# Another order and other banks for the up products, and halved first down products, in the MLP stage of a hybrid decoder layer

## What is computed

```python
h = rms_norm(x, norm_mlp[l])
x = x + jnp.square(jax.nn.relu(h @ w_up[l])) @ w_down[l]
```

## Time and profile before

| | us |
|---|---|
| median of 2 runs | 889.94 (889.81 to 890.07) |
| profiled execution | 885.3 |
| its span | 883.5 |
| PE busy | 786.3 (89%) |
| DVE, POOL, ACT busy | 535.6, 472.9, 370.2 |
| mean granted clock of PE | 0.944 |

### The profile page before, as it was taken

The page is one execution under the profiler, slowest core; times in us unless marked ns, Lnnn a source line. Parts: engine busy times, 40 slices in busy tenths (PEclk is TensorE's granted clock), DMA queues, the critical chain, the costliest instruction groups (busy, mean ns, idle before and its releaser), DMA issues.

```text
span 883.5 us, 13102 instructions
## 1 busy us (share of the span) xinstructions
PE 786.3 (89%) x5122; PEld 670.4 (76%) x5122; DVE 535.6 (61%) x697; ACT 370.2 (42%) x604; POOL 472.9 (54%) x328
## 2 busy tenths in 40 slices
PE   8999999999999999999867789777897778977788
PEld 6888779887878887888767767676677766877666
DVE  6793788666855663547844766266652666325666
ACT  5202834564145554224254643345423453244531
POOL 5666446674566665666962625444344343553444
PEclk9999999999999999999979789898898988989889
DMA  7253222324211003324874968659486585965734
GB/s 275 74 177 110 97 75 73 119 97 167 96 49 48 26 24 120 143 96 167 235 194 110 244 177 209 153 145 239 127 212 148 142 240 124 231 163 125 191 62 129
DMA packets 37647, 124.40 MB, mean 141 GB/s; under 512 B 4259, under 2 KB 5035, under 8 KB 37588
## 3 DMA queue, kind: packets, MB, share of 16 engines
q1 hardware_dynamic: 24108, 81.06, 26.1%
q0 software_dynamic: 9360, 34.08, 21.0%
q10 hardware_dynamic: 4120, 8.44, 2.7%
HBM read 119.35 MB, written 5.26 MB: 141 GB/s over the span
## 4 chain that ended last, share of the span: by engine, by line
PE 66%; DVE 15%; ACT 7%; DMA 5%; issue 5%; POOL 1%; ACTq 1%; DVEq 0%; SPq 0%; POOLq 0%
PE bank L664 10%; PE bank L666 10%; PE bank L665 10%; DVE wsp L2079 4%; PE bank L1170 4%; PE bank L1171 4%; PE bank L1172 4%; DMA wraw<-in_w 4%; PE bank L1138 3%; ACT wsp L1551 3%; PE bank L1140 3%; PE bank L1141 3%; PE bank L1011 2%; PE bank L1044 2%; PE bank L1056 2%
## 5 line engine op out<-in xcount | busy, mean ns | idle before, releaser
L1138 PE MATMUL bank<-ghi,wsp 128*128 128x256 f32 x432 | 133.0, 308 | 63.0 <-DVE v_up L2096 23.8
L592 POOL TENSOR_TENSOR wsp<-wraw,wsp 128x1024 fp32r<-128x1024 f32 x44 | 118.2, 2731 | 99.9 <-ACT wsp L1551 99.8
L1551 ACT ACTIVATE wsp<-wraw 128x1024 fp32r<-128x1024 f32 x86 | 90.7, 1055 | 163.4 <-PE bank L1172 73.6
L515 POOL TENSOR_TENSOR wsp<-wraw,wsp 128x1024 fp32r<-128x1024 f32 x60 | 148.0, 2466 | 5.0
L664 PE MATMUL bank<-hhi,wsp 128*128 128x512 f32 x352 | 140.9, 400 | 2.0 <-DVE hlo L1651 1.1
L1138 PEld LDWEIGHTS bank<-ghi,wsp 128*128 128x128 f32 x432 | 92.0, 213 | 65.7 <-issue 52.1
L666 PE MATMUL bank<-hhi,wsp 128*128 128x512 f32 x352 | 137.4, 390 | 0.0
L665 PE MATMUL bank<-hlo,wsp 128*128 128x512 f32 x352 | 137.1, 390 | 0.0
L1140 PE MATMUL bank<-glo,wsp 128*128 128x256 f32 x432 | 130.7, 302 | 0.0
L1141 PE MATMUL bank<-ghi,wsp 128*128 128x256 f32 x432 | 130.4, 302 | 0.0
L513 POOL TENSOR_SCALAR wsp<-wraw 128x1024 fp32r<-128x1024 f32 x60 | 65.3, 1088 | 119.9 <-PE bank L666 107.1
(11 more groups left out here) (332 smaller groups left out, 1476.6 us busy)
## 6 DMA issues: line engine op xcount, KB each, us to landing
wraw<-in_w SPq DMA_DIRECT2D x126, 512.0 KB, 4.1
wraw<-in_w POOLq DMA_DIRECT2D x49, 512.0 KB, 7.3
raw<-in_w SPq DMA_DIRECT2D x16, 512.0 KB, 5.5
raw<-in_w POOLq DMA_DIRECT2D x15, 512.0 KB, 7.2
bias_skewed<-bias_lines ACTq DMA_DIRECT2D x1, 2048.0 KB
bias<-bias_skewed ACTq DMA_DIRECT2D x1, 2048.0 KB, 8.9
out<-fin SPq DMA_DIRECT2D x8, 256.0 KB, 2.1
x<-in_xT SPq DMA_DIRECT2D x3, 512.0 KB, 6.2
```

The lines of the kernel that those rows point to most:

```text
L515: pool.tensor_tensor(wlo[:, two, :], wraw[:, raw, :], whi[:, two, :].bitcast(F32), ALU.subtract).then_inc(w_split, 1)
L592: pool.tensor_tensor(lo, place, hi.bitcast(F32), ALU.subtract).then_inc(pool_low, 1)
L1138: pe.matmul(out_, hi[:, c], ghi[:, k, g, :], start=start and pp == 0 and k == 0, stop=False, skip_group_check=True)
L1551: act.activation(split_slot(n)[0], place, ACT.Copy).then_inc(split_hi, 1)
```

## The change

- The up products of a half go in the order S1, A11, S3, S2, A12, A22, S4, into banks named Z, X, W, Y, X, Y, Z. T3's product has a bank of its own (W) and T4's adds to Y. Z and W change places between the halves (banks 0 and 2). The sums become v = p1 - Y, p1 = W - v, u22 = p1 + Z, u12 = p1 + Y, s4 = v - Z; the first three come together after unit 3.
- The steps that need sums of the X chain (S1, S2, S4) are now units 0, 3 and 6.
- The down products begin with three products by their first halves (b11, t1, t3), then their second halves; the other four stay as they were. `take_off` counts in `c_read`, and the first down product waits for that count.
- The last group of forms is split in two (`GROUPS`), and VectorE's low parts of the forms of half 0 are moved into its work for half 1, those of half 1 behind it.
- POOL adds the next quarter's first X sum ahead of the last down sums, and Y later; it takes other low parts. VectorE makes only one low part of the next quarter before it keeps t4.
- At the start ScalarE issues the first three loads instead of SyncE and makes the high parts of steps 0 to 3, which POOL did (L590); POOL makes the low parts of steps 0 and 1 between the last `wo` weights. The low part of the activations' forms (`g_low`) comes ahead of the sum of squares for n of 4 or more.

```diff
-UP_FORMS = ["A11", "S1", "S2", "A12", "S3", "A22", "S4"]
-UP_PRODUCTS = [("X", "B11", True), ("Z", "T1", True), ("Y", "T2", True), ("X", "B21", False), ("Y", "T3", False),
-               ("W", "T4", True), ("Z", "B22", False)]
+UP_FORMS = ["S1", "A11", "S3", "S2", "A12", "A22", "S4"]
+UP_PRODUCTS = [("Z", "T1", True), ("X", "B11", True), ("W", "T3", True), ("Y", "T2", True), ("X", "B21", False),
+               ("Y", "T4", True), ("Z", "B22", False)]
-GROUPS = [(0, 1), (1, 3), (3, 7)]
+GROUPS = [(0, 1), (1, 3), (3, 5), (5, 7)]
+DOWN_UNITS = ([(m, half) for half in range(2) for m in range(3)] + [(m, half) for m in range(3, 7) for half in range(2)])
-GROUP_OF = {"u11": 0, "s1": 1, "s3": 1, "s4": 2, "s2": 2, "u12": 2, "u22": 2}
+GROUP_OF = {"u11": 0, "s1": 1, "s3": 1, "s4": 2, "s2": 2, "u12": 3, "u22": 3}
-POOL_LOWS = [0, 3, 4, 5, 7, 10, 11, 12] + [UP_N + 2 * SPLITS.index(part) + half for part in ("b11", "b22", "b21")
-                                            for half in range(2)]
+POOL_LOWS = [1, 2, 4, 5, 8, 9, 11, 12] + [UP_N + DOWN_UNITS.index((SPLITS.index(part), half))
+                                          for part in ("b11", "b22", "b21") for half in range(2)]
...
-        up_bank = dict(zip("XYZW", (bank[0], bank[1], bank[2], bank[3])))
+        up_bank = [dict(zip("ZXWY", (bank[0], bank[1], bank[2], bank[3]))), dict(zip("ZXWY", (bank[2], bank[1], bank[0], bank[3])))]
...
-            sp.wait_ge(w_used, AT["ab7"] + 1)
-            load_raw(0, 0, "X", up_chunk(0, 0, "O1"))
-            sp.dma_start(s1_first[:], up_chunk(0, 0, "O1")).then_inc(first_landed, 16)
-            load_raw(0, 0, "Y", up_chunk(0, 0, "O1"))
...
+                if c == N_STRAIGHT - 6:
+                    pool.wait_ge(first_landed, 16)
+                    pool.dma_start(s1_first[:], up_chunk(0, 0, "O2"), accum_op=ALU.add).then_inc(first_added, 16)
+                if c == N_STRAIGHT - 5:
+                    add_to(0, 0, "X", 1, up_chunk(0, 0, "O2"))
+                if c == N_STRAIGHT - 4:
+                    add_to(0, 0, "Y", 1, up_chunk(0, 0, "E1"))
+                if c == N_STRAIGHT - 3:
+                    low(0)
+                if c == N_STRAIGHT - 2:
+                    low(1)
...
                     n = STEPS * q + 7 * d
-                    low(n)
-                    if n == 0:
-                        low(1)
-                        low(2)
-                    else:
-                        after_low(n + 1, q, d, "X", 2, up_chunk(q, d, "E1"))
                     if n:
-                        low(n + 3)
-                    after_low(n + 2, q, d, "X", 3, up_chunk(q, d, "E2"))
+                        after_low(n, q, d, "X", 2, up_chunk(q, d, "E1"))
+                        low(n + 1)
+                    low(n + 2)
                     if n == 0:
                         low(3)
                     if d == 0:
-                        first_up_sums(q, 1)
+                        up_pair(q, 1, "X")
+                        up_pair(q, 1, "Y")
+                    after_low(n + 3, q, d, "X", 3, up_chunk(q, d, "E2"))
+                    if d:
+                        down_pair(q, 0, "b12")
+                        down_pair(q, 0, "x")
                     low(n + 4)
                     low(n + 5)
...
+                for half in range(2):
+                    after_low(step_of(q, "t3", half), q, half, "x", 2, part_chunk(q, "b11", half))
+                    low(step_of(q, "b22", half))
+                if not end:
+                    up_pair(q + 1, 0, "X")
+                for half in range(2):
+                    after_low(step_of(q, "t2", half), q, half, "x", 3, part_chunk(q, "b21", half))
+                    if end and half == 0:
+                        pool.wait_ge(b_read, 3 * q + 1)
+                        end_sum(sum5, ALU.subtract)
+                    if not end and half == 1:
+                        up_pair(q + 1, 0, "Y")
+                    low(step_of(q, "b21", half))
...
+                if i == 1 and big:
+                    pe.wait_ge(relu_d, 4 * big - 2)
+                if i == 2 and d:
+                    pe.wait_ge(up_sums, 5 * big)
+                if i == 2 and q and not d:
                     pe.wait_ge(b_read, 3 * q)
-                if i == 3:
+                if i == 4:
                     pe.wait_ge(p1_kept, big + 1)
-                done = {1: 5 * big, 2: 5 * big - 3, 4: 5 * big + 1, 5: 5 * big - 1, 6: 5 * big + 3}.get(i, 0)
-                if done > 0:
-                    pe.wait_ge(up_sums, done)
+                if i == 5:
+                    pe.wait_ge(up_sums, 5 * big + 1)
+                if i == 6:
+                    pe.wait_ge(up_sums, 5 * big + 3)
...
+                for m, half in DOWN_UNITS:
+                    if m == 2 and half == 0:
+                        pe.wait_ge(up_sums, 5 * (2 * q + 2))
+                    if m == 3 and half == 0:
+                        pe.wait_ge(c_read, 2 * q + 1)
...
+                if n in (2, 3, 6, 7):
+                    high({2: 0, 3: 1, 6: 2, 7: 3}[n])
...
+                    if n:
+                        high(n + 3)
                     high(n + 4)
                     if d:
                         high_of_group(q, 0, 1)
+                    act.wait_ge(w_used, used(n + 1))
+                    if big:
+                        act.wait_ge(up_sums, 5 * big - 1)
+                    act.activation(p1_up[:], up_bank[d]["X"][:], ACT.Copy).then_inc(p1_kept, 1)
                     high(n + 5)
                     if d:
                         high_of_group(q, 0, 2)
                     high(n + 6)
+                    if d:
+                        high_of_group(q, 0, 3)
+                    if big == 0:
                         act.wait_ge(m_stat, 1)
...
-                low(n + 4)
+                low(n + 3)
+                if d:
+                    low_of_group(q, 0, 1)
+                    low_of_group(q, 0, 2)
+                low(n + 6)
+                dve.wait_ge(w_used, used(n + 3))
                 dve.wait_ge(p1_kept, big + 1)
                 dve.tensor_tensor(v_up[:], p1_up[:], y_[:], ALU.subtract).then_inc(up_sums, 1)
-                low(n + 6)
-                low_of_group(q, d, 0)
-                dve.wait_ge(w_used, used(n + 4))
-                dve.tensor_tensor(p1_up[:], y_[:], p1_up[:], ALU.subtract).then_inc(up_sums, 1)
+                dve.wait_ge(up_sums, 5 * big + 1)
+                dve.tensor_tensor(p1_up[:], w_[:], v_up[:], ALU.subtract).then_inc(up_sums, 1)
...
+                low(n + 7)
+                if d:
+                    low_of_group(q, 0, 3)
                     low(n + 8)
+                low_of_group(q, d, 0)
+                if d:
+                    low(n + 9)
...
-                low_of_group(q, d, 1)
-                low_of_group(q, d, 2)
...
+                low_of_group(q, 1, 1)
                 low(step_of(q, "t1", 1))
-                low(step_of(q, "t3", 0))
+                low(step_of(q, "t3", 1))
+                low_of_group(q, 1, 2)
+                low_of_group(q, 1, 3)
                 keep(q, "b11", "a", sum_v, a_read, first=q == 0, scaled=False)
-                low(step_of(q, "t3", 1))
                 keep(q, "t1", "c", sum5, c_read)
...
                 if not end:
-                    low(n + STEPS + 1)
-                    low(n + STEPS + 2)
+                    low(n + STEPS)
                     keep(q, "t4", "b", sum4, b_read)
```

More of the change, by code:

```diff
@@ L627, in _ @@
                     if d == 0:
[L628 removed]
+                        up_pair(q, 1, "X")
[4 more added lines that the diff above has]
+                        down_pair(q, 0, "x")
                     low(n + 4)
                     low(n + 5)
[L631 to L643 removed]
+                down_pair(q, 1, "b12")
+                low(step_of(q, "b11", 0))
+                down_pair(q, 1, "x")
+                low(step_of(q, "b11", 1))
+                for half in range(2):
[11 more added lines that the diff above has]
+                    low(step_of(q, "b21", half))
             end_sum(sum4, ALU.add)
@@ L1526, in _, with high @@
             link(act.activation(minus_g, g_mlp, ACT.Copy, scale=-1.0))
+            act.wait_ge(w_used, AT["ab7"] + 1)
+            act.dma_start(s1_first[:], up_chunk(0, 0, "O1")).then_inc(first_landed, 16)
+            for role in ("X", "Y"):
+                s = slot_of(0, 0, role)
+                act.dma_start(raw_slots[s], up_chunk(0, 0, "O1")).then_inc(m_landed[s], 16)
+            def high(n):
+                if n >= STEPS * QUARTERS:
+                    return
+                place, there = raw_of(n)
+                act.wait_ge(*there)
+                act.wait_ge(w_used, slot_free(n))
+                act.activation(split_slot(n)[0], place, ACT.Copy).then_inc(split_hi, 1)
             for n in range(KT):
@@ L2064, in _ @@
                 g_forms(n)
+                if n >= 4:
+                    g_low(n)
                 dve.wait_ge(x2_sq, 4 + n + 1)
```

191 lines of the change are left out of this document (74 added, 117 removed).

## The result

The changed kernel takes 853.89 us (median of 2 runs, 853.23 to 854.55) against 889.94: a ratio of 0.9595 (95% interval 0.9554 to 0.9636), 36 us less. The profiled execution took 853.2, its span 851.1 (883.5 before), with PE 780.8 us busy (92%) and a mean granted clock of 0.964 (0.944).

A forecast was written before the change was run, and what follows sets the result against it. The MLP stage was taken as bound by PE's waits: a quarter of 79.0 plus 16.6 pauses and 5.8 slow clock, 101.4 against 108.8. Three quarters save 22.2, the first loses 4.0: 18.2 less, 871 us, range 854 to 888.

The forecast's parts named there:

- A: New pause before unit 5 of half 0, v waiting behind S4's low part and the third X sum: 3.0 us.
- E: New pause before b22, waiting for keep t1 behind the forms' last low parts on VectorE: 4.4 us.
- P1: Old pause of 6.46 us before unit 1 of half 0, behind keep t4; forecast to go.
- P3: Old pause of 3.73 us before unit 1 of half 1, waiting for s4's sum; forecast to go, 0.3 left.
- P5: Old pause of 3.76 us before the second half of t1, behind the forms' low parts; forecast to go.
- B: New pause before unit 3 of half 1, S2's low part late on VectorE after meeting GpSimd's low parts: 5.4 us.
- P4: Old pause of 6.29 us before unit 4 of half 1, waiting for v behind a forms' low part and `take_off`.
- C and D: Estimated pauses: 1.4 us before unit 5 of half 1; 2.4 before the second halves of b11, t1 and t3.
- R1: Rival: VectorE's and GpSimd's low parts mostly don't meet; quarter 92, total 844, or 857 with half the meetings gone; chance 0.21.
- R2: Rival: sums share DMA engines with SP's loads, the third X sum lands 3 us later; total 881; chance 0.18.
- R3: Rival: pauses only move, the quarter stays at 108 to 109; total 889 to 893; chance 0.10 shared with another rival.
- R4: Rival, slower: the third X sum lands 17 us after issue, delaying v; total 896; chance 0.07.

The follow-up runs named there:

- e16: Changed kernel with whole first down products and the low parts of half 0's forms back where the kernel before had them: 859.1 us.
- e12: Changed kernel with the low parts of s1, s3 and the third group of half 0's forms back ahead of half 1's first low parts: 867.9 us.
- e9: Changed kernel with the moves of e3, e6 and e8 together: 807.5 us.
- e2: Kernel before, with VectorE keeping t4 ahead of the low part of the next quarter's S2: 885.7 us.
- e15: Kernel before, with the low parts of half 0's second and third group of forms behind v and S4's low part of half 1: 889.8 us.
- e13: e9 with GpSimd's low part of unit 4 of half 1 ahead of three sums for the down products: 817.6 us.
- e11: Kernel before with two moves: keep t4 ahead of S2's low part, and S4's low part behind the sum u22: 904.5 us.
- e3: Changed kernel with v, W - v and u22 of half 0 ahead of S4's low part on VectorE: 835.2 us.
- e6: Changed kernel with half 0's third X sum issued ahead of half 1's first two sums: 831.3 us.
- e8: Changed kernel with the low part of the third group of half 1's forms behind the keeps of b11 and t1: 838.5 us.

## Why the prediction was wrong

The sign, the new long pauses A and E and the end of P1, P3 and P5 were right; the sum of a quarter, and so the total, was too high. The largest term that failed is pause B. By its steps:

- **P1 and P3 go, A comes.** Held: A is 3.6 to 4.0 (3.0 taken, 1.8 to 4.7 allowed) with the chain as forecast; the sum was 11.3 on its way where 10 was taken. v was ready 18.2 after unit 0 began (553.35 to 571.54), where the working had 16.5; that the 3.0 came close owes something to its being taken 1.1 above the working's own 1.9. In e16 the same exchange is 11.2 us of P1 to P3 for an A of 3.8 to 6.4, some 17 of its 28 us over three quarters.
- **B, the step that failed.** 5.4 was forecast and 1.35 to 1.47 measured. The working put u11's low part behind both of GpSimd's, 5.0 long; VectorE got in between them and it took 2.49 (2.48 and 2.49 in the other quarters). The other 1.4 is slow clock: the five units after A took 16.0 in place of 14.6, so unit 3 was due later, while VectorE's chain to S2's low part, which starts at v and not at PE's units, was not. I charged the slow clock behind A to the quarter and still let B be due at full speed. Behind B there was one that I had not, 2.2 before unit 4 of half 1: GpSimd's low part behind three DMA issues. B and this are 3.6 for P4's 6.3. B took over the larger part of P4 in e12 (4.6 to 5.0), where the forms' low parts stand in its chain again.
- **C and D.** 1.4 and 2.4 taken, 0 (1.0 in one quarter) and 0.9 measured, inside their bounds but both at the lower end.
- **E.** 4.4 taken, 4.18 measured. The terms as written don't add up to 4.4: with both low parts at 3.4 the sum is 6.7 (6.8 + 1.2 + 1.4 - 2.7), with one of them 4.5, and one is what the trace has (4.76 for both). So the working said two meetings and its number had one; that it fits is in part luck.
- **Slow clock.** 5.8 taken; 98.65 - 79.0 - 12.5 leaves 7.1. A pause of 3.8 brings it too, and in two of three quarters so did one of 2.2 soon after one of 1.5 (0.83 over 10 us, in the windows above).
- **The quarter.** 98.65 against 101.4: pauses 4.1 less (B 4.0, C and D 2.9 and E 0.2 less, A 0.8 and the pause before unit 4 2.2 more), clock 1.3 more. Over three quarters that is 8 of the 14 by which the two profiled executions differ from the forecast (-32.4 against -18.2).
- **The first quarter.** -4.0 forecast, -0.7 measured. The pause at the transposes came (4.26 for 4), and so did E (4.18). But S2's low part behind the eight issues cost 4.02 in place of 7, and the pause for v, 4.87 in before, fell to 1.95, where I let the rest stay. In all the first quarter came out 3.3 of the 14 better: up to its first down product the two kernels take the same (506.99 and 506.94).
- **The last quarter.** I let it save what the others save; it saved 12.7, 2.5 more. The end of the kernel gave none of it: its down products take 0.4 more than before. The saving is in the up products (13.2 less, 12.2 and 11.9 in the two quarters ahead), where no slow clock followed the pauses before units 3 and 4, and in down products that lose less (0.4 for 1.3 and 2.5).
- **The base.** The medians differ by 36.1, the profiled executions by 32.1.
- **The rivals.** R1 (the meetings mostly don't happen) was right about B's size and wrong about E: the quarter lies between its 92 and the forecast's 101.4, and 853.9 a little below its half-way case of 857. Its DMA limit was wrong: e9 has 84.8 at a share of 0.88. R2's 13 us for the third sum was not seen, 11.3 was. R3's way of going wrong, pauses that only move, is what e2 and e15 did in the old order. R4's late sum didn't come (11.3, and it needed 15).

In the Trainium skill (SBUF — State Buffer, "SBUF: two separate sides") whichever of the two starts first gets the pair for the whole instruction. The trace agrees: at B VectorE waited out one instruction of GpSimd (2.49 at 576.96, 0.68 for the same low part without company), and so it did in e13 (4.75 for two in place of 2.36). Who is next when GpSimd has another one ready isn't settled by this: in the earlier trace rows and in e15 VectorE came only behind the second, at B between the two. What decides between these stays open, and B hung on it with 2.5 us.

## What to carry to other kernels

Where a weight goes through sum, split and product in series, try first to spread its consumers evenly over the schedule. In the old order (units 1, 2 and 6) moves in the queues mostly shifted their pause to the next sum (2 and 10 us gained, nothing, and 18 us lost by e11's two); with the sums three products apart, moves of the same kind paid 15 to 23. That the spacing makes this difference is what the traces suggest; it was never changed by itself.

Moves that remove the same pause should not be added up: e3, e6 and e8 alone gave 18.7, 22.6 and 15.4, together 56.7, and e9 with all three gives 46 (e3 and e6 were not run together without e8). Count also the slow clock behind a pause: in e8 it was most of the gain. Work a pause's due time out at the clock that will hold then, not at full speed.

For VectorE's low parts a DMA issue of GpSimd was good company (2.35 for two) and a low part of GpSimd's was bad (4.75): look at what a moved instruction will stand beside, not only at what it stands behind.

## What the runs showed of the hardware

- Two of VectorE's low parts (128 x 1024 each) took 2.35 beside GpSimd's DMA issues, 4.75 beside one of its low parts.
- Beside two low parts of GpSimd that followed each other at once, one of VectorE's got in between (changed kernel, 2.49), and another waited for both (e15: 8.94 for two, of which the second waited until 603.8, when GpSimd was done, and then took 2.3).
- One and the same accumulating DMA, the third X sum, landed 11.3 after its issue as the third of a burst and 6.0 as the first (e6).
- Over the 7 us behind each of the pauses A and E in the changed kernel (3.6 to 4.2 long) the granted clock was 0.58 to 0.78. A pause's length doesn't tell what comes after it when it is shorter: one of 2.2 that came 3 us after one of 1.4 or 1.5 was followed by 0.83 over 10 us in quarters 1 and 2 of the changed kernel and by 1.00 in its quarter 3; in e9 the same pair was followed by 1.00, and a single pause of 1.74 a quarter later by 0.65:

```profile
576.89:586.89 10.00, 10.00 (x78) 9.78 (x79) 6.14 (x6) 7.65 (x10) 7.25 (x4) 1.00 1.04 261
...
656.68:661.10 4.42, 4.42 (x24) 4.13 (x24) 2.21 (x2) 0.00 (x0) 4.18 (x5) 0.65 0.59 86
```

In the first of these windows DMA's share was 1.04 and the clock full, in the second 0.59 and the clock low: DMA's load did not lower the clock.
